# Expert pairs sorted once ahead of the expert loop, outputs stored as pair rows and fetched back by token

## The chip, the cores and the metric

One of the eight cores of a Trainium2 chip runs the whole program. The metric is device time in microseconds for one launch, taken as the median of several. Everything is float32; a few matmuls are done on float32 values split into a high and a low part in the narrower fp32r type.

## The reference, cut to what matters

Two layers work on 256 tokens of width 1024. Each has a token mixer and a channel mixer; the second layer's channel mixer is the one that is changed. It sends every token to the best two of eight experts, each a SwiGLU of inner width 3584:

```python
logits = t @ w_router + b_router
top_val, top_idx = lax.top_k(logits, 2)
gates = jax.nn.softmax(top_val)
# the 512 (token, expert) pairs are sorted by expert; then, for each expert's rows xblk:
yb = (silu(xblk @ w_gate_e[e]) * (xblk @ w_up_e[e])) @ w_down_e[e]
y[token] += gate_of_pair * yb
x = x + gate * rmsnorm(y, g_norm[1, 3])      # last norm and residual
```

Each expert's weights are 42 pieces of 1 MB (14 stages of gate, up and down), so all eight are 336 MB, read once.

## The kernel before

The first layer, the second mixer and the norm ahead of the experts keep the activations feature-major: `xT`, `hT` hold features on partitions and tokens along them. SyncE issues nothing but weight loads, in a fixed order, through a ring: 7 slots of 1 MB up to the experts, 14 slots (`ring_e`) for them. A slot is loaded again when `gu_full` or `down_done` says that its last reader is through (L650 and `last_use`).

**Routing.** PE computes the router's logits (L1103), transposes `hT` to token-major banks (L1108), and ScalarE copies these to `tok`. VectorE finds the two best experts of each token, the gates, and a token's rank within its expert by five small matmuls with a triangular matrix (L1114 to L1118). `cnt` then holds the number of tokens of each expert; `pos`, `Mm` and `Gm` hold ranks, membership and gates.

**The expert loop** is a real loop (`Fori`) of eight turns on PE, ScalarE and VectorE. Each engine loads `cnt[e]` into a register (L551 is the test that follows) and goes through nested `If`s to one of six bodies, for at most 32, 64, 128, 160, 192 or 256 tokens. A body of PE does, in this order:

- gather: VectorE has made a one-hot matrix `oh` (and one times the gates, `ohg`); PE multiplies `tok` by `oh` into four banks (L1146) and transposes `ohg` (L1152); ScalarE and VectorE copy the results to `mixT` and `gPT`;
- 14 stages, each once or twice (a block of 128 tokens and a rest): gate and up into a PG bank (L1176 for blocks under 128 rows, L1182 for 128), SiLU on ScalarE (L1253), the product on VectorE (L1955), a transpose by matmul (L1193), its copy (L1960), and the down product into Y (L1203). They are software-pipelined: the gate and up of a unit, the transpose of the one before it, the down product of the one before that;
- scatter: ScalarE and VectorE copy Y to `yeK` (L1253, L1966); PE multiplies `yeK` by `gPT` into four banks (L1226), and VectorE adds these to `yacc`, feature-major (L1971).

ScalarE's helper records all its operations as L1253. A semaphore wait stands ahead of each use of a bank or buffer.

**The end**: squares of `yacc`, their sum over partitions by matmul (L712, L717, L722), the root on GpSimd (L1992), gain and residual (L1567, L1571, L1997), 16 transposes to token-major (L1241), a copy to `tok`, and two stores by SyncE.

## Time and profile before

| what | value |
|---|---|
| median of 3 runs | 2094.73 us (2093.11 to 7076.81) |
| profiled execution | 2095.57 us, span 2093.8 us |
| PE busy | 1811.4 us, 87% of the span |
| VectorE, ScalarE, GpSimd busy | 443.5, 299.3, 43.1 us |
| bytes moved | 484.86 MB, mean 232 GB/s |
| expert loop | from 849.7 us to 2069.6 us |

The spans of the views are microseconds from the first instruction. "PE" is a matmul, "PEld" the load of its stationary operand; a float32 matmul call is recorded as two instructions. "issue" is time in which an engine waits for nothing that the profile shows. In the order of the loop the eight experts took the bodies for 32, 32, 128, 64, 160, 32, 192 and 64 tokens (read from the shapes of their matmuls). Here they are called E0 to E7. A "boundary" is the stretch from the end of an expert's last down product to the start of the next expert's first gate product.

### The profile page before, as it was taken

The numbers are of one execution on the slowest core, as the hardware profiler recorded it, in microseconds if no ns is written. First come the engines' busy times: TensorE is split into PE (matmuls) and PEld (weight loads), VectorE is DVE, ScalarE is ACT, GpSimd is POOL, SyncE is SP. The second block draws the span as 40 slices with busy tenths as digits, with TensorE's granted clock in tenths as the row PEclk, the third lists the DMA queues.
The fourth block names the chain that finished last, engine by engine and source line by source line (L and its number), as shares of the span: only waits on it lengthen the run. The fifth ranks groups of instructions, "written<-read, shape, count | busy, mean of one in ns | idle before, by whom it ended". The sixth has DMA issues, their size and how long they took to land.

```text
span 2093.8 us, 32178 instructions
## 1 busy us (share of the span) xinstructions
PE 1811.4 (87%) x13586; PEld 1349.1 (64%) x13587; DVE 443.5 (21%) x971; ACT 299.3 (14%) x585; POOL 43.1 (2%) x48
## 2 busy tenths in 40 slices
PE   3998979999899897665679979699997689999796
PEld 2776759999776676554467755477665466666453
DVE  1152235555415222111010011110011010000112
ACT  1222133333212211101000000100000010000101
POOL 0010000000001001000000000000000000000000
PEclk7997689999998767878789989799997889999797
DMA  6732357555342135599977759946463974444393
GB/s 235 286 121 80 149 188 286 183 183 189 131 147 110 75 155 223 240 419 402 420 316 288 297 205 417 388 164 240 196 241 159 420 318 181 181 181 181 112 418 139
DMA packets 75639, 484.86 MB, mean 232 GB/s; under 512 B 11872, under 2 KB 16236, under 8 KB 17516
## 3 DMA queue, kind: packets, MB, share of 16 engines
q1 hardware_dynamic: 71616, 478.02, 57.5%
q10 hardware_dynamic: 3756, 3.39, 0.6%
q8 instruction: 155, 2.54, 0.5%
q14 instruction: 112, 0.92, 0.1%
HBM read 480.33 MB, written 1.05 MB: 230 GB/s over the span
## 4 chain that ended last, share of the span: by engine, by line
PE 82%; issue 7%; DMA 5%; DVE 3%; ACTq 1%; ACT 1%; POOL 1%; SPq 0%; DVEq 0%; POOLq 0%
PE PG L1182 14%; PE Y L1203 13%; PE PG L1176 11%; DMA arena<-in_experts 5%; PE Y L796 4%; PE TRB L1193 3%; PE Y L804 3%; PE TRB L736 3%; PE Y L1049 3%; PE PG L760 3%; PE PG L762 3%; PE PG L761 3%; PE PG L1226 2%; PE TRB L1146 1%; PE TRB L1226 1%
## 5 line engine op out<-in xcount | busy, mean ns | idle before, releaser
L1960 DVE COPY arena<-TRB 128x64 f32<-128x64 f32 (+2 forms) x140 | 42.6, 305 | 835.4 <-PE TRB L1193 835.4
L1253 ACT ACTIVATE arena<-PG 128x256 f32<-128x256 f32 (+2 forms) x168 | 57.8, 344 | 1019.8 <-PE PG L1176 513.8
L1176 PE MATMUL PG<-ring,mixT 128*32 128x128 f32 (+1 forms) x2640 | 159.8, 320 | 28.2 <-issue 26.5
L1176 PE MATMUL PG<-arena,mixT 128*32 128x128 f32 (+1 forms) x2288 | 146.2, 336 | 36.3 <-issue 36.3
L1203 PE MATMUL Y<-arena 128*32 128x256 f32 (+2 forms) x896 | 171.6, 489 | 3.4 <-issue 3.4
L1176 PEld LDWEIGHTS PG<-ring,mixT 128*32 128x32 f32 (+1 forms) x2640 | 119.3, 124 | 75.3 <-issue 51.3
L1182 PE MATMUL PG<-ring,mixT 128*128 128x256 f32 x720 | 160.7, 381 | 1.3 <-DVE mixT L1943 1.3
L1176 PEld LDWEIGHTS PG<-arena,mixT 128*32 128x32 f32 (+1 forms) x2288 | 108.6, 131 | 78.5 <-issue 58.5
L1182 PEld LDWEIGHTS PG<-ring,mixT 128*128 128x128 f32 x720 | 135.4, 190 | 29.3 <-issue 11.9
L1182 PE MATMUL PG<-arena,mixT 128*128 128x256 f32 x624 | 139.9, 380 | 0.0
L760 PE MATMUL PG<-h_parts,parts 128*128 128x256 f32 x448 | 126.8, 283 | 10.0 <-DVE parts L1854 10.0
L1182 PEld LDWEIGHTS PG<-arena,mixT 128*128 128x128 f32 x624 | 117.0, 189 | 26.5 <-issue 10.2
L1203 PE MATMUL Y<-ring,arena 128*32 128x256 f32 (+2 forms) x672 | 127.9, 482 | 1.9 <-issue 1.9
L762 PE MATMUL PG<-h_parts,parts 128*128 128x256 f32 x448 | 126.8, 283 | 0.0
L761 PE MATMUL PG<-h_parts,parts 128*128 128x256 f32 x448 | 125.6, 280 | 0.0
L1146 PE MATMUL TRB<-arena,tok 128*128 128x128 f32 (+2 forms) x128 | 32.3, 446 | 89.3 <-issue 89.3
L1203 PEld LDWEIGHTS Y<-arena 128*32 128x32 f32 (+2 forms) x896 | 60.8, 134 | 71.5 <-issue 58.5
L1854 DVE TENSOR_TENSOR parts<-ring,parts 128x2048 fp32r<-128x2048 f32 x42 | 95.9, 2292 | 25.7 <-ACT parts L1253 25.7
L796 PE MATMUL Y<-hT,ring 128*128 128x256 f32 x416 | 95.3, 390 | 0.0
L760 PEld LDWEIGHTS PG<-h_parts,parts 128*128 128x128 f32 x448 | 85.4, 191 | 10.8 <-DVE parts L1854 10.4
L1146 PEld LDWEIGHTS TRB<-arena,tok 128*128 128x128 f32 x128 | 30.0, 330 | 94.0 <-issue 94.0
L1193 PEld LDWEIGHTS TRB<-con,arena 128*128 128x128 f32 (+1 forms) x448 | 62.8, 191 | 42.5 <-issue 40.5
(295 smaller groups left out, 2230.4 us busy)
## 6 DMA issues: line engine op xcount, KB each, us to landing
ring<-in_experts SPq DMA_DIRECT2D x168, 1024.0 KB, 9.1
arena<-in_experts SPq DMA_DIRECT2D x168, 1024.0 KB, 15.5
ring<-in_weights SPq DMA_DIRECT2D x116, 1024.0 KB, 6.3
ring<-in_weights SPq DMA_DIRECT2D x4, 512.0 KB, 4.0
tok<-in_x ACTq DMA_DIRECT2D x1, 1024.0 KB, 13.7
result<-tok SPq DMA_DIRECT2D x2, 512.0 KB, 2.8
ring<-in_weights SPq DMA_DIRECT2D x2, 432.0 KB, 6.2
arena<-in_w_ukv ACTq DMA_DIRECT2D x2, 384.0 KB, 4.2
```

What stands on the lines that cost most here:

```text
L736: last = mm(bank[32 * c:32 * c + 32, 0:SW], ccol[:, k, :], ring[:, slot_of[u], k, :], start=(k == 0), stop=(k == KD - 1))
L760: mm(out_, w_hi[w][:, c], x[0], start=first, stop=False, skip_group_check=True)
L761: mm(out_, w_hi[w][:, c], x[1], start=False, stop=False, skip_group_check=True)
L762: return mm(out_, w_lo[w][:, c], x[0], start=False, stop=last, skip_group_check=True)
L796: last = mm(bank_part, ring[:, s, k, c:c + m], hT[:, k, :], start=(k == 0), stop=(k == KD - 1))
L1146: last = mm(bank[:, j * T:j * T + w], tok[:, b, k * P:(k + 1) * P], oh[:, b, 0:w], start=(b == 0), stop=(b == TB - 1))
L1176: last = mm(bank[i * m:(i + 1) * m, 0:width], x[:, k, :], w[c // SW][:, k, c % SW:c % SW + width], start=(k == 0), stop=(k == KD - 1))
L1182: last = mm(bank[:, i * SW:(i + 1) * SW], x[:, k, :], w[i][:, k, :], start=(k == 0), stop=(k == KD - 1))
L1193: last = mm(tr[u % 2][:, f * P:(f + 1) * P], actK[r, u % 2, f * P:(f + 1) * P], ident[r, :], start=True, stop=True)
L1203: last = mm(o, actT[:, u % 2, f, 0:m], w[:, f, c:c + width], start=(s == 0 and f == 0), stop=(s == STAGES - 1 and f == 1))
L1226: last = mm(bank[:, q * T:(q + 1) * T], yeK[0:m, j, k * P:(k + 1) * P], gPT[0:m, j, :], start=(j == 0), stop=(j == len(bl) - 1))
L1854: V.tensor_tensor(w_lo[d % SPLITS], ring[:, slot_of[slot_of_dense(d)], :, :].rearrange("p k c -> p (k c)"), w_hi[d % SPLITS].bitcast(F32), ...
```

## The change

The pairs are ranked over all experts at once: `first[e]` is an exclusive sum of the counts, `slot` a pair's row among 512. The sorted activations `xs` (feature-major, 8 x 512 columns) are made before the loop by one product of `htok_hi` and `htok_lo` (the token-major activations split in two) with the 0/1 matrix `sel`, 32 matmuls of 512 columns, copied out by ScalarE and VectorE. In the loop GpSimd copies the expert's 256 columns of each of the 8 feature tiles from `xs` to `xe` (the buffer of `mixT`), once the expert before has done its last gate product. There is no gather, no transposed gate matrix and no scatter; the down outputs go to `yeK` and from there, by a DMA that ScalarE issues at a register's offset, to a DRAM scratch `ypairs`. `yeK` lies in `hT`'s buffer, and the first down product of an expert waits until the expert before has been copied out. After the loop GpSimd fetches two rows for each token with four indirect DMAs; ScalarE and VectorE weight and add them, and the last norm and residual are done token-major. The router's product runs in four column groups with a second small product that adds them. Slots of the ring, the six bodies and the loads of weights stay.

```diff
@@ tensor
-            for b in range(TB):
-                for k in range(KD):
-                    ...
-                    last = mm(bank[:, b * NE:(b + 1) * NE], hT[:, k, b * P:(b + 1) * P], wr[:, k, :], ...)
+            for k in range(KD):
+                pe.wait_ge(h_ready, 3 * KD + k + 1)
+                g = 32 * (k % 4)
+                last = mm(bank[g:g + 32, 0:T], wr[:, k, :], hT[:, k, :], start=(k < 4), stop=(k >= 4))
...
+            bank = take_tr("logit")
+            pe.wait_ge(*tr_done("router"))
+            for b in range(TB):
+                last = mm(bank[:, b * NE:(b + 1) * NE], s4[:, b * P:(b + 1) * P], strip_sum, start=True, stop=True)
...
             pe.wait_ge(htok_ready, 4)
+            pe.wait_ge(hlo_ready, 4)
+            pe.wait_ge(sel_ready, TB)
+            for k in range(KD):
+                f = slice(k * P, (k + 1) * P)
+                for b in range(TB):
+                    mm(xg_banks[k], htok_hi[:, b, f], sel[:, b, :], start=(b == 0), stop=False)
+                    last = mm(xg_banks[k], htok_lo[:, b, f], sel[:, b, :], start=False, stop=(b == TB - 1))
+                last.then_inc(xg_full, 1)
+            pe.wait_ge(xs_ready, KD)
+            pe.wait_ge(table_ready, 1)
+            pe.sem_inc(ye_ready, 2)
             with pe.Fori(0, NE) as e:
...
-                    pe.wait_ge(hot_ready, e * 1 + 1)
-                    for i in range(4):
-                        ...  (gather: mm(bank, tok, oh))
-                    for b in range(TB):
-                        ...  (transpose of ohg)
+                    pe.wait_ge(xe_ready, e + 1)
...
                         pe.wait_ge(at_ready, at_own(e, n, u))
+                        if s == 0:
+                            pe.wait_ge(ye_ready, e * 2 + 2)
...
-                    pe.wait_ge(ye_ready, e * 2 + 2)
-                    for i in range(4):
-                        ...  (scatter: mm(bank, yeK, gPT))
-            stats("post", 3, 7)
...
+            for b in range(TB):
+                for k in range(KD):
+                    last = nc.tensor.transpose(xtok_banks[b][k // 4][...], xT[:, k, b * P:(b + 1) * P], ident)
+            pe.wait_ge(ye_ready, 2 * NE + 2)
+            pe.wait_ge(diag8_ready, KD)
+            for k in range(KD):
+                last = mm(Y[:, k // 4, ...], ones[:, :], diag8[:, k, :], start=True, stop=True)
@@ scalar
+            for k in range(0, KD, 2):
+                ae.wait_ge(xg_full, k + 1)
+                run(xs[:, k * PAIRS:(k + 1) * PAIRS], xg_banks[k], ACT.Copy).then_inc(xs_ready, 1)
             with ae.Fori(0, NE) as e:
                 n_tok = ae.value_load(cnt[0:1, bass.ds(e, 1)], min_val=0, max_val=T)
+                start = ae.value_load(first[0:1, bass.ds(e, 1)], min_val=0, max_val=PAIRS)
...
                     ae.wait_ge(down_done, e * FT + 2 * FT)
+                    for b in range(TB):
+                        ae.wait_ge(y_stored[b], e * 16 + 16)
                     ...  (yeK copies)
                     last.then_inc(ye_ready, 1)
+                    ae.wait_ge(ye_ready, e * 2 + 4)
+                    for j, m in blocks(n):
+                        ae.dma_start(ypairs[bass.ds(start + j * P, m), :], yeK[0:m, j, :]).then_inc(y_stored[j], 16)
...
+            for b in range(TB):
+                ae.wait_ge(y_back[b], 32)
+                run(y1[:, b, :], y1[:, b, :], ACT.Copy, scale=gt2[:, b, 0:1]).then_inc(y1_scaled, 1)
+            for b in range(TB):
+                ae.wait_ge(y_summed, b + 1)
+                run(mixT[...], y2[:, b, :], ACT.Square, accum_out=msq[:, b:b + 1]).then_inc(ysq_ready, 1)
@@ vector
+            V.tensor_tensor(Mm, oh[:, :, 0, :], oh[:, :, 1, :], ALU.add).then_inc(routed, 1)
+            for q in range(4):
+                ve.wait_ge(htok_ready, q + 1)
+                V.tensor_tensor(htok_lo[...], Y[:, q, :], htok_hi[...], ALU.subtract).then_inc(hlo_ready, 1)
+            ...  (counts, scan to `upto`, pos, cnt, first, ohp, slot: some ten small operations)
+            for b in range(TB):
+                mark(V.tensor_scalar(sel[:, b, :], iota, slot[:, 2 * b:2 * b + 1], None, ALU.is_equal))
+            for b in range(TB):
+                V.scalar_tensor_tensor(sel[:, b, :], iota, slot[:, 2 * b + 1:2 * b + 2], sel[...],
+                                       ALU.is_equal, ALU.add).then_inc(sel_ready, 1)
...
+            for k in range(1, KD, 2):
+                V.tensor_copy(xs[:, k * PAIRS:(k + 1) * PAIRS], xg_banks[k]).then_inc(xs_ready, 1)
...
-                    one_hot(e + 1)
-                    for i in range(6, 10):
-                        ...  (yacc += bank)
-            post(3)
+            for b in range(TB):
+                V.scalar_tensor_tensor(y2[:, b, :], y2[:, b, :], gt2[:, b, 3:4], y1[:, b, :], ALU.mult, ALU.add)
+            ...  (mean square)
+            for b in range(TB):
+                ...  (y1 = y2 * rstd * gain, two halves; y1 += xT transposed, two halves)
@@ gpsimd
+            for k in range(KD):
+                G.tensor_scalar(diag8[:, k, :], ident, gg[:, 3, k:k + 1], None, ALU.mult).then_inc(diag8_ready, 1)
+            with po.Fori(0, NE) as e:
+                start = po.value_load(first[0:1, bass.ds(e, 1)], min_val=0, max_val=PAIRS)
+                po.wait_ge(gu_full, e * FT + FT)
+                src = xs[:, bass.ds(start, KD * PAIRS)].rearrange("p (k s) -> p k s", k=KD)
+                G.tensor_copy(xe[:, :, :], src[:, :, 0:T]).then_inc(xe_ready, 1)
+            for b in range(TB):
+                po.wait_ge(y_stored[b], 16 * NE + 16)
+            for b in range(TB):
+                for c, to in enumerate((y1, y2)):
+                    po.indirect_dma_start(to[:, b, :], None, ypairs[0:PAIRS, :], ...).then_inc(y_back[b], 16)
+            for b in range(TB):
+                G.tensor_tensor(rstd[:, b:b + 1], msq[:, b:b + 1], half[:, 0:1], ALU.pow).then_inc(end_rstd, 1)
```

## Rows read from the trace of the kernel before

**Rows 1.** Stretches: from:to, length, busy PE, PEld, DVE, ACT, POOL, PEclk, DMA share, GB/s.
```profile
880.00:930.00 50.00, 32.38 (x594) 24.11 (x598) 3.64 (x14) 1.89 (x7) 0.00 (x0) 0.80 1.01 420
1070.00:1210.00 140.00, 140.00 (x585) 106.91 (x586) 10.58 (x29) 6.28 (x14) 0.00 (x0) 1.00 0.73 284
1240.00:1330.00 90.00, 89.07 (x646) 52.14 (x645) 12.58 (x36) 7.80 (x19) 0.00 (x0) 0.98 0.89 366
1700.00:1940.00 240.00, 239.50 (x1221) 154.88 (x1221) 23.89 (x62) 12.67 (x32) 0.00 (x0) 1.00 0.47 185
```

**Rows 2.** Chain that ended last: start, length, what; from E0 to E2.
```profile
1008.25 25.91 DMA arena<-in_experts
...
1043.28 1.91 PE Y L1203 x32
...
1050.08 10.43 issue
1060.51 3.77 PE TRB L1146 x16
...
1069.76 10.26 PE PG L1182 x46
```

**Rows 3.** The same chain, from the end of E6 to the start of E7.
```profile
1941.51 5.53 PE Y L1203 x16
...
1956.07 9.20 PE PG L1226 x16
...
1980.55 4.50 PE PG L1176 x39
```

**Rows 4.** Groups by line over the expert loop: busy us, mean ns, idle before by releaser.
```profile
L1146 PE MATMUL TRB<-arena,tok 128*128 128x128 f32 (+2 forms) x128 | 32.3, 446 | 89.3 <-issue 89.3
...
L1253 ACT ACT_TABLE_LOAD x15 | 19.2, 1283 | 117.7 <-issue 89.6 <-PE PG L1176 20.4 <-PE PG L1182 7.6
```

**Rows 5.** Timeline from the router to E0's first gate product.
```profile
826.60 6.97 PE L1103 MATMUL TRB<-wr,hT 128*128 128x8 f32 x32 [1.67 <-ACT hT L1253]
...
837.10 2.06 ACT L1253 ACTIVATE tok<-Y 128x512 f32<-128x512 f32 x4 [2.35 <-PE Y L1108]
...
849.68 3.78 PE L1146 MATMUL TRB<-arena,tok 128*128 128x128 f32 x16 [10.98 <-issue]
...
856.61 3.66 PE L1176 MATMUL PG<-ring,mixT 128*32 128x128 f32 x123 [0.40 <-DVE mixT L1943]
...
858.76 0.86 SPq L650 DMA_DIRECT2D ring<-in_experts  x2
```

**Rows 6.** Timeline of boundaries, with the idle time before each: E3 to E4, E5 to E6.
```profile
1329.58 0.69 DVE L1966 COPY arena<-Y 64x512 f32<-64x512 f32 x1 [3.25 <-PE Y L1203]
...
1343.90 1.28 ACT L1253 ACT_TABLE_LOAD   x1 [13.74 <-issue]
...
1351.86 4.63 PE L1146 MATMUL TRB<-arena,tok 128*128 128x160 f32 x16 [16.70 <-issue]
...
1693.33 5.15 PE L1146 MATMUL TRB<-arena,tok 128*128 128x192 f32 x16 [8.81 <-issue]
```

**Rows 7.** The chain between E4 and E5, VectorE's way to its next body.
```profile
1584.39 2.93 issue
...
1587.45 3.42 issue
```

**Rows 8.** Stretches: the fp32r matmuls of the dense layer; before E0.
```profile
400.00:500.00 100.00, 100.00 (x847) 100.00 (x846) 53.22 (x53) 36.49 (x30) 0.00 (x0) 1.00 0.51 182
840.00:850.00 10.00, 0.32 (x1) 0.33 (x2) 0.40 (x2) 1.28 (x1) 0.00 (x0) 0.56 0.05 11
```

**Rows 9.** Groups of GpSimd by form.
```profile
L2016 POOL COPY arena<-scr 32x1536 f32<-32x1536 f32 x2 | 2.9, 1456 | 57.7 <-DVE scr L1697 57.7
```

**Rows 10.** The chain at the end: E7's last down products.
```profile
2060.72 3.61 PE Y L1203 x16
```

**Rows 11.** DMA issues: queue, count, KB each, median us to landing.
```profile
result<-tok SPq DMA_DIRECT2D x2, 512.0 KB, 2.8
```

More of the change, by code:

```diff
@@ L69, in const_table @@
     t[:, C_MK:C_MK + P] = np.where(i[None, :] < CHUNK, 0.0, NEG)
-    t[:, C_IOTA:C_IOTA + T] = np.arange(T)
+    t[:, C_IOTA:C_IOTA + PAIRS] = np.arange(PAIRS)
+    for e in range(NE):
+        t[e:P:32, C_SEL + e] = 1.0
     for m in range(CR // 2):
@@ L238, in rs_names, with build @@
     return names
-def build(nc, ap, out):
+def build(nc, ap, out, ypairs):
     uses = weight_uses()
@@ L386, in build @@
         h_hi, h_lo = h_parts[:, 0, :, :], h_parts[:, 1, :, :]
-        yacc = cut("ffn", KD, T)
+        sel_at = top["ffn"]
+        sel = parts[:, sel_at:sel_at + TB * PAIRS].rearrange("p (b s) -> p b s", b=TB)
+        diag8 = cut("ffn", KD, P)
         sgK = cut("ffn", 2, SW)
@@ L399, in build @@
         gt2 = cut("ffn", TB, 4)
-        oh1 = cut("ffn", TB, NE)
-        oh2 = cut("ffn", TB, NE)
-        Gm = cut("ffn", TB, NE + 1)
-        Mm = cut("ffn", TB, NE + 1)
-        pos = cut("ffn", TB, NE + 1)
+        oh = cut("ffn", TB, 2, NE)
+        ohp = cut("ffn", TB, 2, NE)
+        Mm = cut("ffn", TB, NE)
+        pos = cut("ffn", TB, NE)
+        total = cut("ffn", NE)
+        upto = cut("ffn", NE)
+        zero8 = cut("ffn", NE)
+        slot = cut("ffn", 2 * TB)
+        msq = cut("ffn", TB)
+        rstd = cut("ffn", TB)
+        xe = mixT
+        yeK = hT.rearrange("p k t -> p (k t)").rearrange("p (b d) -> p b d", b=TB)
+        htok_hi, htok_lo = (h_parts[:, i, :, :].rearrange("p k t -> p (k t)").rearrange("p (b d) -> p b d", b=TB) for i in range(2))
+        y1 = scr.rearrange("p k t -> p (k t)").rearrange("p (b d) -> p b d", b=TB)
+        y2 = tok
         ring_e = [ring[:, (n_before + i) % SLOTS, :, :] for i in range(SLOTS)] + [cut("ffn", KD, SW) for _ in range(SLOTS_E - SLOTS)]
@@ L502, in build @@
         htok_ready = sem("htok_ready")
-        hot_ready = sem("hot_ready")
-        ax_full = sem("ax_full")
-        ax_free = [sem(f"ax_free{i}") for i in range(4)]
+        hlo_ready = sem("hlo_ready")
+        table_ready = sem("table_ready")
+        sel_ready = sem("sel_ready")
+        xg_full = sem("xg_full")
+        xs_ready = sem("xs_ready")
+        pad_zero = sem("pad_zero")
+        xe_ready = sem("xe_ready")
+        y_stored = [sem(f"y_stored{i}") for i in range(TB)]
+        y_back = [sem(f"y_back{i}") for i in range(TB)]
+        diag8_ready = sem("diag8_ready")
+        end_full = sem("end_full")
+        y1_scaled = sem("y1_scaled")
+        y_summed = sem("y_summed")
+        ysq_ready = sem("ysq_ready")
+        msq_ready = sem("msq_ready")
+        end_rstd = sem("end_rstd")
         tp_full = sem("tp_full")
@@ L607, in tr_done @@
             return tr_free[TR.bank(name)], TR.before(name) + 1
-        tr_before_experts = [TR.before(x) + 1 for x in ("router", "rank")]
-        if TR.bank("router"):
-            tr_before_experts.reverse()
         block = ctx.enter_context(nc.Block())
```

262 lines of the change are left out of this document (115 added, 147 removed).

## The prediction

> **What bounds the kernel now.** I read the stretches first. In the loop two things alternate. Inside E2, E3, E4, E6 and E7 PE is busy without a break while the DMA engines are not full: 140.00 of 140 us at a DMA share of 0.73 in E2, 89.07 of 90 at 0.89 in E3 [rows 1]. Inside E0, E1 and E5, the bodies for 32 tokens, PE is busy 32.38 of 50 us and the DMA engines all the time, at 420 GB/s [rows 1]; there the chain of waits passes through the landing of weights, 25.91 us at one go [rows 2]. At that rate an expert's 42 pieces take 42 x 1.0486 / 0.42 = 105 us. The loop of eight takes some 1214 us, 8 x 105 would be 840: outside the small experts the weights are no bound.
>
> Next I read the chain at the boundaries. From the end of E1's last down product (1045.19) to E2's first gate product (1069.76) pass 24.6 us [rows 2]; from E6's (1947.04) to E7's (1980.55) 33.5 [rows 3]. The six boundaries from E1/E2 to E6/E7 take 24.6, 24.4, 30.2, 33.6, 23.9 and 33.5, together 170.2 us. PE-bound experts follow or precede each of them, or (E5) one that can't load ahead further than its 14 slots, so a boundary's length is on the path. The seventh, E0/E1, isn't: the DMA engines are full from E0's start to E1's end.
>
> Of a boundary, one part is PE idle for "issue": 89.3 us over eight entries to a body [rows 4], of which 11.0 before E0 [rows 5] and 15.9 before E1, so 62.5 in the six, 8.8 to 16.7 each except one of 4.5 [rows 6]. It is the way through the loop's end, the register load and the nested tests: on VectorE between E4 and E5 the chain shows four stops, the first two of 2.93 and 3.42 us and the others like them, one for each jump [rows 7]. The rest, 170.2 - 62.5 = 107.7 us, is gather, scatter and their copies.
>
> The Trainium skill (Runtime: NRT & Kernel Launch, Instruction fetch mechanics) says that a taken branch out of the two pages held makes the sequencer fetch the target first; the four stops agree. Its page Advanced Engine Details and Errata (Control Flow Timing) gives about 51 ns for a branch and 108 ns for a compare and branch; if that were all, a boundary would be some 12 us shorter than in my sum and the time about 1950. Every entry in the trace speaks against it.
>
> **The boundaries after the change.** The jumps stay: same loop, same six bodies, on PE, ScalarE and VectorE. PE starts its jumps as soon as the last down product is issued. Its bounds are the idle times seen, 8.8 and 16.7 us [rows 6]. The lower ones flatter it: PE's sequencer had queued the scatter's products (up to 9.20 us of them [rows 3]) and was jumping while they ran, and now only the last down product, 1 to 3.5 us, covers it. ScalarE, which had no such lead, took 13.74 us from its last copy to its first instruction of the next body [rows 6], and 89.6 over the seven boundaries [rows 4], 12.8 each. I take 12.5 us for PE. Then gate products start at once, on a PE that has idled: its clock is 0.56 over such a gap [rows 8], and the first 16 gather products took 3.77 us at 1.2 GHz before the rate went up [rows 2]. Up to now the gather paid for that; now the gate products lose half of it, 1.9 us.
>
> ScalarE's new work: wait for both halves of `yeK`, issue one or two DMAs (0.43 us each, as SyncE's issues: 0.86 for two [rows 5]), a second register load. It leaves about 2 us after PE's last product, needs 12.8 us for its jumps and 1.28 for a table [rows 6], so SiLU 0 can be done about 16.5 us after it. PE needs it only for the transpose of unit 0, behind two units of gate products: 12.5 plus 4 to 14 us. A lateness of 0.5 us on average goes into the sum (0 for the 128-row bodies, up to 3 for the small). VectorE is no later.
>
> GpSimd's copy of `xe` moves 2048 elements a partition: 1456 ns for 1536 [rows 9] give 2 us. It starts at the last gate product, at least 4.5 us before the last down product ends, so 12.5 + 4.5 us cover it; without that cover it would cost 2 us a boundary. The waits for `ye_ready` before the first down product and for `y_stored` before the copies (from the store of the expert before, 80 us or more back) cost nothing for the same reason. The stores, 2 MB in all, are 5 us of DMA time, nearly all where the engines have room.
>
> New length: 12.5 + 1.9 + 0.5 = 14.9, times six 89.4. **Saved: 170.2 - 89.4 = 81 us.** At 8.8 a boundary it would be 103, at 16.7 it would be 56.
>
> Does this turn back into waiting for weights? E3 needs 3 pieces per 6 us stage against 2.4 arriving, with 14 ahead: 14 + 2.4 x 13 = 45 for 42. E4 then begins with about 8 instead of 14, at 14.7 us a stage: enough. E5 starts with a full ring as now. Nothing is given back.
>
> **Ahead of the loop.** The DMA engines are idle, share 0.05 [rows 8], until E0's first gate product frees a slot (858.76 [rows 5]), and E0 and E1 run on the weights from there: whatever is added here shifts everything. Router: 6.97 us of 32 recorded instructions [rows 5] become 8 calls in four column groups, bounded by the arrival of `hT`, about 3.5 us less; the transposes, unchanged, and two small products bring the logits to VectorE at 834.4, 0.8 later than now. One-hots and `routed`: 836.4. ScalarE's four copies (2.06) end at 838; VectorE subtracts the low parts, 4 x 0.69 us (0.69 for 512 columns on VectorE [rows 6]), till 839.3; some ten small operations till 841.1; `sel`, four of 512 columns at 0.6 to 0.7, till 843.8. Then 32 products of 512 columns. 847 fp32r instructions of 256 columns took 100 us [rows 8], 0.118 each, so 0.236 at full clock and 0.47 at half. About 4 us at half, the rest at full: 9.4 us (bounds 7.5 and 15), and 0.6 for the last copy: 854. Only now PE and the others enter the loop: 10.5 us of jumps, as before E0 now [rows 5], under which GpSimd's eight small operations and first copy (4 us) are hidden. E0's first gate product: 864.5 instead of 856.6, and the first slot free 1.7 us later for the half clock. **Added: 9.5 us** (bounds 5 and 16).
>
> **The end.** Now 2093.8 - 2064.3 = 29.5 us follow the last down product [rows 10]. New: copies 0.7; issue and landing of the store 3.3 (2.8 for 512 KB [rows 11]); four indirect DMAs of 512 KB on GpSimd. None is in the trace: bounds 2.8 us if they overlap wholly, 4 x 2.8 + 4 = 15 if they don't; I take 7.5, as their bytes need 5 us at 420 GB/s. Then scale 1.0, square 2.0, VectorE's sum 1.2, root 0.7 and five or six 512-wide pairs at 1.4 on two blocks, 6 in all, store 3.2. Sum 25.6: **saved 4 us** (from -8 to 9). The Trainium skill (DMA: Bandwidth & Descriptors, Anatomy of one DMA) has about 2.0 us plus bytes at 436 GB/s for a DMA of GpSimd; 2 MB would be 6.8 us by it, an estimate, and the sum would hardly move.
>
> **Sum.** The profiled execution took 2095.57 us, 0.8 above the median. 2095.6 - 81 + 9.5 - 4 = 2020.
>
> **Rivals.**
> - *The jumps get longer.* Scatter and gather spread the engines' jumps apart; now three engines jump within 2 us of one another, fetch at once, and the slowest decides, at 16.7 plus lateness of ScalarE up to 3. Six boundaries at 19: 2020 + 25 = 2045. For: entries of 15.9 and 16.7 stand where the DMA engines were busy. Against: 8.8 stands there too. 20%.
> - *The jumps get shorter*: PE's queue covers more, 8.8 a boundary: 1998. 10%.
> - *The gain comes back as waiting for weights* in E3 to E5, 30 us of it: 2050. Against: the count of pieces. 6%.
> - *Slower: the row fetches.* If GpSimd builds each row's descriptor one by one, the end grows with 512 rows. It decides from (2020 to 2137) 117 us, 0.23 us a row; at 0.25 the time is 2020 + 128 - 7 = 2141. No row here has an indirect DMA, so it can't be excluded. 3%.
> - *My forecast*: 2000 to 2042, 61%.
>
> **Numbers.** 2020; range 1992 to 2052, from the short jumps to the long ones with the bounds of prologue and end. A measurement tells about 2% from no change, 2053 here. Faster: 0.61 + 0.10 + 0.15 of the long jumps + 0.04 = 0.90; same 0.07; slower 0.03.
>
> **What would show it.** Right: no 30 us boundaries; six of 11 to 18 us with a single "issue" stop; clock 0.5 over the first 4 us of each body; weights' landing still ends the waits in E0, E1, E5; first slot freed near 868. Wrong: PE waiting for ScalarE or VectorE at unit 0 by more than 3 us, stops well outside 8.8 to 16.7, waits for weights in E3 or E4, more than 40 us after the last down product.

## The result: 2.4% faster, 26 us less than forecast

The changed kernel takes 2046.16 us (median of four runs, 2040.29 to 2046.67), the kernel before beside it 2094.4: a ratio of 0.9755, 95% interval 0.9741 to 0.9769 (the two medians by themselves divide to 0.977; one execution of the kernel before, of 7076.81 us, stands outside the ratio). The forecast was 2020 in 1992 to 2052, and "faster". The profiled execution took 2046.35 us, its span 2044.6 against 2093.8.

### Where the span went

Four instants cut both traces: the router's first product, E0's first gate product, the end of the last down product, the end of the span.

| stretch | before | after | change | predicted |
|---|---|---|---|---|
| start to router | 826.6 | 831.6 | +5.0 | 0 |
| router to E0's first gate product | 30.0 | 36.2 | +6.2 | +7.9 |
| E0's first gate to E7's last down product | 1207.7 | 1150.5 | -57.2 | -79 |
| of it: the six boundaries | 170.3 | 101.8 | -68.5 | -81, with the slower start of each body |
| of it: inside the bodies, and E0/E1 | 1037.4 | 1048.7 | +11.2 | +1.7 |
| last down product to the end | 29.5 | 26.3 | -3.2 | -4 |

Chain of waits after, start, length, what; the lines that answer to [rows 2, 3], then those of the other boundaries:

```profile
1061.97 10.75 issue
1072.72 15.83 PE PG L1189 x64
...
1225.75 13.36 issue
1239.11 9.31 PE PG L1183 x64
...
1324.94 18.75 issue
...
1551.82 18.14 issue
...
1653.48 13.58 issue
1667.06 8.62 PE PG L1189 x32
...
1913.20 19.68 issue
1932.88 8.88 PE PG L1183 x64
```

Where there were a stop, a gather, copies, and at the end a scatter ([rows 2, 3]: 24.6 and 33.5 us), there is one stop and nothing else. Two of the lines are shorter than the boundary, because at its start the chain runs through the landing of the last weights (E1/E2, E5/E6); from product to product the six take 13.2, 13.4, 18.8, 18.1, 18.7 and 19.7 us, mean 17.0.

Waits of PE after, over the loop (868 to 2018 us): engine, line, what for: total, times, longest:

```profile
PE PG L1183 <- issue: 152.6, 33, 20.1
PE PG L1189 <- issue: 50.6, 3, 18.8
PE Y L1212 <- issue: 3.9, 3, 1.6
PE TRB L1200 <- DVE arena L1954: 0.4, 1, 0.4
PE Y L1212 <- DMA arena<-in_experts: 0.2, 1, 0.2
```

That is the whole list. PE hardly waits for ScalarE, VectorE or GpSimd anywhere in the loop, and outside "issue" it shows one wait for weights, of 0.2 us. (In the 32-token bodies a wait for a slot's weights hides under "issue", as in the 62.8 us of L1176 before; the chain shows it as a DMA.)

Timeline after, the boundary E3/E4 of [rows 6]: start, length, engine, line, operation, and in brackets the idle time before:

```profile
1326.01 0.62 ACTq L1492 DMA_DIRECT2D ypairs<-hT  x1
1342.10 1.28 ACT L1246 ACT_TABLE_LOAD   x1 [16.38 <-issue]
...
1343.70 9.95 PE L1189 MATMUL PG<-ring,mixT 128*128 128x256 f32 x32 [18.75 <-issue]
```

From its last copy ScalarE does nothing for 16.4 us but issue its store and jump, and it stands in the next body 1.6 us before PE. Before, the same way took it 13.74, and PE, which could start jumping while the scatter ran, 16.70 [rows 6].

Timeline after, from the router to the first freed slot, the lines that answer to [rows 5]:

```profile
831.64 3.76 PE L1123 MATMUL TRB<-hT,wr 128*32 128x256 f32 x16 [1.67 <-ACT hT L1246]
...
839.72 2.04 ACT L1246 ACTIVATE h_parts<-Y 128x512 fp32r<-128x512 f32 x4
...
845.41 1.41 DVE L1927 SCALAR_TENSOR_TENSOR parts<-con,arena,parts 128x512 fp32r<-128x512 f32 x2
...
847.04 0.77 PE L1153 MATMUL PG<-parts,h_parts 128*128 128x512 f32 x1 [4.06 <-issue]
...
856.07 0.39 PE L1154 MATMUL TRB<-parts,h_parts 128*128 128x512 f32 x1
...
857.35 4.68 POOL L2062 TENSOR_SCALAR arena<-con,gg 128x128 f32<-128x128 f32 x8 [28.86 <-DVE arena L1944]
861.98 1.89 POOL L2067 COPY mixT<-arena 128x2048 f32 x1
...
867.82 5.48 PE L1183 MATMUL PG<-ring,mixT 128*32 128x128 f32 x128 [11.36 <-issue]
871.65 2.71 SPq L671 DMA_DIRECT2D ring<-in_experts  x4
```

Measured from the router's first product: router 3.76 us long (6.97 before, [rows 5]; I said 3.5 less), `sel` ready after 15.2 (said 17.2), 32 gather products in 9.4 us (said 9.4, about 4 us of it at the lower clock: they start every 0.42 us up to 851.0 and every 0.23 behind it), then 11.36 us from the last of them to E0's first gate product (said 11.1). GpSimd's eight small operations and first copy end 6.5 us after they began (said 4). The slot is freed 40.0 us after the router, 32.2 before: +7.9, said +9.5.

Chain of waits after, the end, the lines behind [rows 10]:

```profile
2014.70 3.61 PE Y L1212 x16
...
2019.36 2.99 DMA ypairs<-hT
...
2022.64 1.21 POOL scr L2072
2024.15 0.94 POOL tok L2072
...
2026.64 5.65 DMA tok<-ypairs,row_of
2032.31 1.16 ACT scr L1246
```

A row fetch of 128 rows is issued in 0.94 us (the first 1.21); the last lands 5.65 us behind the start of its issue; four take 9.7 us, overlapped. I took 7.5.

Stretches after (from:to, length, busy PE, PEld, DVE, ACT, POOL, PEclk, DMA share, GB/s): the inside of E0, E2, E3 and E6, as in [rows 1], and the first 4 us of E4:

```profile
895.00:945.00 50.00, 32.03 (x575) 24.73 (x576) 3.64 (x14) 1.88 (x7) 1.28 (x1) 0.80 1.01 420
1085.00:1225.00 140.00, 140.00 (x568) 103.28 (x567) 10.25 (x27) 4.99 (x13) 1.90 (x1) 1.00 0.75 299
1245.00:1325.00 80.00, 79.94 (x584) 43.80 (x580) 10.07 (x28) 6.55 (x15) 1.90 (x1) 1.00 1.00 409
1343.70:1347.70 4.00, 4.00 (x10) 3.19 (x11) 0.00 (x0) 0.00 (x0) 0.00 (x0) 0.50 1.03 420
...
1700.00:1900.00 200.00, 200.00 (x1000) 128.13 (x999) 17.95 (x46) 8.74 (x23) 0.00 (x0) 1.00 0.46 182
```

PE is busy 140.00 of 140 us in E2 and 79.94 of 80 in E3, where the DMA share is now 1.00 instead of 0.89: the margin I counted for E3 is used up, and no wait has come of it. In E0 the weights are the bound as before, at 420 GB/s. A body begins at a granted clock of 0.50, the level of 1.2 GHz, as forecast.

### The profile page after: what moved, and what is told of

The parts are those of the page before. It is cut to its first block, busy times and chain, and to the rows that moved or that the text cites. A ratio compares the mean times of both kernels' runs of the same rounds, so it can differ in the third digit from the quotient of the medians.

```text
span 2044.6 us, 31233 instructions
## 1 busy us (share of the span) xinstructions
PE 1716.0 (84%) x13162; PEld 1278.3 (63%) x13163; DVE 409.3 (20%) x887; ACT 283.9 (14%) x553; POOL 62.8 (3%) x67
## 4 chain that ended last, share of the span: by engine, by line
PE 77%; DMA 8%; issue 8%; DVE 3%; ACT 1%; ACTq 1%; POOL 1%; SPq 0%; POOLq 0%; DVEq 0%
PE PG L1189 15%; PE Y L1212 13%; PE PG L1183 11%; DMA ring<-in_experts 6%; PE Y L817 4%; PE TRB L1200 3%; PE Y L825 3%; PE Y L1070 3%; PE PG L781 3%; PE PG L782 3%; PE PG L783 3%; PE TRB L757 2%; DMA arena<-in_experts 1%; PE Y L783 1%; PE Y L782 1%
## 5 line engine op out<-in xcount | busy, mean ns | idle before, releaser
L1183 PE MATMUL PG<-ring,mixT 128*32 128x128 f32 (+1 forms) x2640 | 171.1, 339 | 113.3 <-issue 113.3
L1183 PEld LDWEIGHTS PG<-ring,mixT 128*32 128x32 f32 (+1 forms) x2640 | 128.5, 133 | 165.5 <-issue 141.7
L1189 PE MATMUL PG<-ring,mixT 128*128 128x256 f32 x720 | 166.7, 391 | 50.6 <-issue 50.6
L1189 PEld LDWEIGHTS PG<-ring,mixT 128*128 128x128 f32 x720 | 139.9, 196 | 81.1 <-issue 61.9
L781 PE MATMUL PG<-h_parts,parts 128*128 128x256 f32 x448 | 128.0, 286 | 10.2 <-DVE parts L1848 10.2
L782 PE MATMUL PG<-h_parts,parts 128*128 128x256 f32 x448 | 127.7, 285 | 0.0
L783 PE MATMUL PG<-h_parts,parts 128*128 128x256 f32 x448 | 127.6, 285 | 0.0
L781 PEld LDWEIGHTS PG<-h_parts,parts 128*128 128x128 f32 x448 | 86.9, 194 | 10.8 <-DVE parts L1848 10.4
L1954 DVE TENSOR_TENSOR arena<-PG,arena 64x128 f32<-64x128 f32 (+2 forms) x140 | 52.1, 372 | 190.1 <-ACT arena L1246 185.5
L1200 PE MATMUL TRB<-con,arena 128*128 128x128 f32 (+1 forms) x448 | 87.6, 307 | 0.4 <-DVE arena L1954 0.4
## 6 DMA issues: line engine op xcount, KB each, us to landing
ring<-in_experts SPq DMA_DIRECT2D x168, 1024.0 KB, 10.5
arena<-in_experts SPq DMA_DIRECT2D x168, 1024.0 KB, 16.3
```

The source lines that it names most:

```text
L781: mm(out_, w_hi[w][:, c], x[0], start=first, stop=False, skip_group_check=True)
L782: mm(out_, w_hi[w][:, c], x[1], start=False, stop=False, skip_group_check=True)
L783: return mm(out_, w_lo[w][:, c], x[0], start=False, stop=last, skip_group_check=True)
L1183: last = mm(bank[i * m:(i + 1) * m, 0:width], x[:, k, :], w[c // SW][:, k, c % SW:c % SW + width], start=(k == 0), stop=(k == KD - 1))
L1189: last = mm(bank[:, i * SW:(i + 1) * SW], x[:, k, :], w[i][:, k, :], start=(k == 0), stop=(k == KD - 1))
L1200: last = mm(tr[u % 2][:, f * P:(f + 1) * P], actK[r, u % 2, f * P:(f + 1) * P], ident[r, :], start=True, stop=True)
```

## The experiments

The question was why the stop at a boundary is 17.0 us on average and not 12.5, and what the whole change is worth apart from it. My theory: a stop is the fetch of code over jumps, back to the head of the loop and through the nested tests to the body; TensorE's sequencer makes it while the products already in its queue run, and in the kernel before these were the scatter's. Rivals: the engines fetch at one another's cost since they jump together; PE waits for another engine; the DMA queues are busy with weights.

"Boundary" in what follows is from the end of the last down product to the next first gate product, "stop" the longest idle time of PE within it. This table is worked out from the matmul records of each profiled execution; us. Two executions of one kernel give the spread of a boundary: 0.3 us at most between after and changed_again, but up to 1.4 between unrolled_early and early_again.

| kernel | E1/E2 | E2/E3 | E3/E4 | E4/E5 | E5/E6 | E6/E7 | six stops | six boundaries |
|---|---|---|---|---|---|---|---|---|
| before | 10.4 | 12.9 | 16.7 | 4.5 | 8.8 | 9.1 | 62.5 | 170.3 |
| no_scatter | 14.3 | 13.3 | 18.3 | 16.3 | 13.2 | 18.4 | 93.8 | 136.8 |
| no_gather | 10.8 | 13.7 | 17.7 | 8.8 | 7.8 | 13.6 | 72.5 | 134.3 |
| before_unrolled | 1.6 | 12.6 | 10.3 | 5.0 | 3.1 | 4.6 | 37.2 | 137.5 |
| after | 13.2 | 13.4 | 18.8 | 18.1 | 18.7 | 19.7 | 101.8 | 101.8 |
| changed_again | 13.2 | 13.4 | 18.5 | 18.4 | 18.5 | 19.6 | 101.6 | 101.6 |
| others_unrolled | 13.3 | 13.2 | 18.3 | 17.5 | 18.4 | 19.6 | 100.3 | 100.3 |
| quarter_weights | 9.9 | 9.8 | 13.2 | 13.8 | 12.5 | 14.4 | 73.6 | 73.6 |
| unrolled | 7.5 | 12.8 | 10.7 | 17.8 | 5.7 | 14.0 | 68.5 | 68.5 |
| warm | 6.5 | 8.3 | 13.8 | 7.7 | 6.3 | 11.2 | 53.7 | 137.1 |
| unrolled_early | 6.2 | 12.8 | 12.3 | 17.3 | 6.4 | 14.0 | 68.9 | 68.9 |
| early_again | 7.5 | 13.6 | 10.9 | 18.1 | 6.2 | 13.9 | 70.2 | 70.2 |
| early_idle6 | 1.6 | 11.4 | 6.5 | 12.0 | 2.3 | 10.3 | 44.2 | 76.1 |

### changed_again: the changed kernel once more

> The changed kernel once more, as the base of this group. Both theories: 2040 to 2047 us. The stretch ahead of the router began 5.0 us later in its first trace than before the change (831.64 against 826.60); if that is the state of TensorE's clock in the first 60 us and not the change, it moves by some us here; if it is the change, it stays at 831 to 832. PE's idle time at the six boundaries: 101.7 us in the first trace (13.2, 13.4, 18.8, 18.1, 18.7, 19.7).

2047.07 us, ratio 0.9763 (0.974 to 0.9787), stops as in the first trace within 0.3 us. The router starts at 828.6 us instead of 831.6. In three profiled executions of kernels with the old code ahead of the router it starts at 826.6 and in a fourth (no_gather) at 828.0, mean 826.9; in nine with the new code (the first trace among them) at 825.6 to 831.6, mean 829.2. So about half of the +5.0 us of the first comparison is that one execution. The means differ by 2.3 us, less than the nine are apart from one another; whether that is the change stays open.

### no_scatter: the kernel before without its scatter

```diff
@@ tensor: ahead of the first down product
+                        if s == 0:
+                            pe.wait_ge(ye_ready, e * 2 + 2)
...
-                    pe.wait_ge(ye_ready, e * 2 + 2)
-                    for i in range(4):
-                        bank = take()
-                        ... last = mm(bank[:, q * T:(q + 1) * T], yeK[0:m, j, ...], gPT[0:m, j, :], ...)
-                        last.then_inc(ax_full, 1)
@@ vector
-                    for i in range(6, 10):
-                        ... V.tensor_tensor(o, o, bank..., ALU.add).then_inc(free, 1)
```

> The kernel before the change without the scatter: the products with gPT and the additions to yacc are left out, gather and all else stay, and the first down product waits for the copies as in the changed kernel. Theory A (the scatter's queued products covered the jumps): PE's stops from E4 to E5 and E6 to E7, 4.5 and 9.1 us before, become 17 to 20 us, the others grow by 1 to 3 us, and of 58 us of scatter at the six boundaries only about 25 to 30 show: 2062 to 2072 us. Theory B (the stops in the changed kernel are longer because three engines jump at one time, and gather still comes ahead of the gates here): also longer, so it tells less here. Theory C (the stops are of fixed length, 10.4 us on average): 2094 - 58 = 2036 us.

2056.56 us, ratio 0.9818 (0.9801 to 0.9834), 5 us under the range of theory A (2062 to 2072). Chain of waits, the boundaries E2/E3 and E4/E5:

```profile
1219.61 13.35 issue
1232.96 3.78 PE TRB L1147 x16
...
1555.03 16.33 issue
1571.37 3.78 PE TRB L1147 x16
```

The boundaries lose 33.5 us and the six stops grow by 31.4 (62.5 to 93.8), in the old kernel, with nothing of the change in it. Where the scatter was longest (E4/E5, E6/E7: 9.20 us for its products, [rows 3]) the stop grows most, 4.5 to 16.3 and 9.1 to 18.4; at E2/E3 by only 0.4. That is the failed term: about half of what was removed (31.4 of 33.5 + 31.4) had been running under a fetch of code. The insides of E2, E3, E4, E6 and E7 are unchanged (151.5, 83.8, 205.6, 245.0, 83.8 us); the gather still comes first and takes the lower clock on itself.

### no_gather: the kernel before without its gather

```diff
-                    for i in range(4):
-                        bank = take()
-                        ... last = mm(bank[:, j * T:j * T + w], tok[:, b, ...], oh[:, b, 0:w], ...)
-                        last.then_inc(ax_full, 1)
@@ scalar, vector
-                    ... the copies of these four banks to mixT
```

> The kernel before the change without the gather's 16 products of tok and their copies; the transposes of the gate matrix and the scatter stay, the experts work on old activations. Theory A (scatter's queue covers the jumps, gather doesn't): PE's stops keep their lengths, 62.5 us in the six boundaries, and what goes is the gather alone, 7 to 8 us per boundary and once ahead of E0, less 1 to 2 us of half clock each: 2094 - 7 x 6 = 2052, range 2045 to 2060 us. Theory B (stops are longer when work behind them is short): PE's stops grow here too, as in the run without scatter.

2074.51 us, ratio 0.9896 (0.9879 to 0.9912): 15 us over the range that I gave (2045 to 2060). The profiled execution is the fastest of the five, 2064.13 us where the other four took 2073.0 to 2075.8, so its trace shows 10 us more of a gain than the time does, and where the others lost these 10 us isn't recorded.

In this trace the boundaries lose 36.0 us and the six stops grow by 10.0 (62.5 to 72.5), 4.3 at E4/E5 and 4.5 at E6/E7, so theory A, by which the stops keep their lengths, holds for the other four boundaries alone. The bodies behind them get longer by 1.8, 2.5, 1.9, 1.5 and 1.5 us (E2, E3, E4, E6, E7): this is the price of beginning at half clock, 1.9 on average, and my 1.9 was right. Together with no_scatter the boundaries lose 33.5 + 36.0 = 69.5 us; in the changed kernel they lose 68.5. The traces' two parts add up to what the change does at a boundary. By the times they can't be added in this way, since no_gather's trace isn't its typical execution.

### warm: 16 idle products behind each expert

```diff
                     ... (after the last down product)
+                    for i in range(16):
+                        mm(PG[:, i % 2, :], ident, con[:, 0:512], start=True, stop=True)
```

> The changed kernel with 16 products of 512 columns, whose results nobody reads, behind the last down product of every expert: 13.7 us of PE work at full clock that lies in PE's queue while its sequencer goes to the next body. Theory A (the jumps run beneath queued work; scatter used to be that cover, and gather the warm-up of the clock): the start of the next gate product doesn't move, PE's real idle time at the six boundaries falls from 102 to 20-35 us, and the first two units of gate products run at full clock where the remaining gap is short: 5 to 15 us gained, 2031 to 2041 us. Theory B (the sequencer can't go on while the queue is that full, or jumps only after the queue is empty): every boundary grows by about 13 us, six of them on the path: 2046 + 80 = 2126 us.

2080.77 us, ratio 0.9932 (0.9916 to 0.9949), 34 us more than the changed kernel and between the two theories (2031 to 2041, and 2126). Timeline of PE at E2/E3:

```profile
1229.61 13.90 PE L1225 MATMUL PG<-con 128*128 128x512 f32 x32
1251.77 8.60 PE L1183 MATMUL PG<-ring,mixT 128*64 128x256 f32 x60 [8.26 <-issue]
```

16 products take 13.7 us. The stop behind them is 5.1 us shorter here (13.4 to 8.3) and 8.0 on average (101.6 to 53.7 over six), from 4.8 at E3/E4 to 12.2 at E5/E6. If the fetch began with the queue dry, it would not be shorter at all; if all 16 ran under the fetch, the boundaries would not have grown, and they grew by 35.5 us. So the queue hides a part of such products. How much it holds can't be told from this: the 16 products also make the code longer, and 32 blocks of it are fetched in the six boundaries where the changed kernel fetches 27 or 28 (what a block is stands under unrolled). My further hope, that the products save the clock, failed: the gate products after them run at a granted clock of 0.51 over the first 4 us and take 8.60 us for 60 records, 0.143 each, against 0.115 once the clock is up (32 of them in 3.67 us).

### others_unrolled: the loop written out on ScalarE, VectorE and GpSimd

```diff
-            with ae.Fori(0, NE) as e:
+            for e in range(NE):
@@ the same on VectorE and GpSimd; TensorE keeps its loop
```

> The changed kernel with the expert loop written out on ScalarE, VectorE and GpSimd but kept on PE. Theory A (each engine's way is its own, and PE's is the one that decides): PE's stops and the time as in the changed kernel, 2044 to 2050 us. Theory B (three engines jump at one time and fetch at each other's cost, or PE waits for the slowest): at least half of the 36 us that writing out all of them gave, 2030 us or less.

2040.99 us, ratio 0.9735 (0.9714 to 0.9756), no different from the changed kernel's 0.9763. DMA queues of the page (packets, MB, share), first of the changed kernel, then of this one:

```profile
q8 instruction: 150, 2.46, 0.5%
...
q14 instruction: 106, 0.87, 0.1%
```

```profile
q8 instruction: 150, 2.46, 0.5%
...
q14 instruction: 58, 0.48, 0.1%
```

### unrolled: written out on all four

```diff
-            with pe.Fori(0, NE) as e:
-                n_tok = pe.value_load(cnt[0:1, bass.ds(e, 1)], min_val=0, max_val=T)
+            for e in range(NE):
+                n_tok = pe.value_load(cnt[0:1, e:e + 1], min_val=0, max_val=T)
@@ and the same on ScalarE, VectorE and GpSimd
```

> The changed kernel with the loop over the experts written out eight times on PE, ScalarE, VectorE and GpSimd (the tests for the six bodies stay, SyncE's loop stays). Theory A (a boundary is a number of fetches of far code, 3 to 6 blocks at about 3.5 us each; the way back to the loop's head is one of them on PE): one fetch less, PE's six stops fall from 102 to about 80 us: 2022 to 2030 us. Theory B (the time is in the register load and the tests themselves, or in waits for the other engines): no change within 0.3%. Theory C (more code, worse fetches): slower by up to 1%.

2010.87 us, ratio 0.9594 (0.9578 to 0.961): the gain is larger than theory A had it (2022 to 2030 us, stops of 80). The six stops fall from 101.6 to 68.5. DMA traffic around the boundary E6/E7 (packets, MB, share of that window), of the changed kernel and of this one:

```profile
q8 instruction: 6, 0.10, 3.0%
```

```profile
q8 instruction: 4, 0.07, 2.6%
```

A packet of q8 is a block of 16 KB. Six blocks of code in a stop of 19.7 us, four in one of 14.0. Over the six boundaries I count 27 blocks in 101.8 us and 19 in 68.5: 3.8 and 3.6 us a block. That is an average (3.2 to 5.7 from boundary to boundary): the packets themselves take 0.9 to 2.4 us, and some start in pairs less than 0.6 us apart. The stop follows the number of blocks fetched, and a third of it goes with the jump back to the loop's head. That third is uneven: 12.8 us at E5/E6 and 7.9 at E3/E4, but 0.6 at E2/E3 and at E4/E5. The rest is the way through the tests to the body, and it depends on which body is left and which entered: 5.7 us (one block) from 32 to 192 tokens, 17.8 (five) from 160 to 32.

### quarter_weights: less traffic beside the fetches

```diff
-                slot = ring_e[i % SLOTS_E].rearrange("p k c -> p (k c)")
+                c = KD * SW if full else KD * SW // 4
+                slot = ring_e[i % SLOTS_E].rearrange("p k c -> p (k c)")[:, 0:c]
@@ the first 14 pieces are still loaded whole
```

> The changed kernel with only the first quarter of every expert weight piece loaded after the first 14 pieces (the products read stale data): the DMA engines are nearly idle at every boundary. Theory A (the stops are a number of fetches of far code, each some 3.5 us, whatever else the DMA engines do): PE's six stops stay within 5 us of 101.6, and only E0, E1 and E5 get shorter, by 25 to 35 us each: about 1950 us. Theory B (fetches wait behind weight pieces of 1 MB): the stops where the DMA engines were full (into E1, E2, E4, E6) shrink by 5 us or more each, the others don't: 1930 us or less.

One execution, 1908.05 us; most of the gain is E0, E1 and E5, which no longer wait for weights (47.2, 48.8, 48.3 us instead of 79.4, 92.2, 78.4). The stops fall to 73.6 us, which is neither theory: they shrink by 28 us and not by under 5, and at all six boundaries (3.3 to 6.2 us) and not only at those with full DMA engines. The blocks are about as many, 28 with five that start within the last microsecond before the stop, 23 without them: 2.6 or 3.2 us a block instead of 3.8.

Two things shrink, about half each. From the first of these fetches to the gate product the six boundaries take 72.0 us instead of 85.7 in the first trace of the changed kernel, and 12.1 of these 13.7 us are at E1/E2, E3/E4 and E5/E6, where the DMA engines were full (share 1.01 to 1.02 over the stop, 0.34 to 0.71 at the other three). The other 14.5 us are fetches that begin earlier against the last down product; why they do stays open. So the DMA queues' load is a third cause, about 28 us of the 102. It was there before the change too. At the three boundaries that are not full the share over the stop is somewhat higher in the changed kernel than in no_scatter (0.71, 0.50, 0.34 against 0.61, 0.42, 0.23), so a small part in the difference isn't excluded.

### unrolled_early and early_again: a later wait, and `diag8` built behind the loop

Both are the written-out kernel with this edit:

```diff
-            pe.wait_ge(xs_ready, KD)
             pe.wait_ge(table_ready, 1)
...
                     pe.wait_ge(xe_ready, e + 1)
+                    pe.wait_ge(xs_ready, KD)
@@ gpsimd: the eight operations that make diag8 moved from ahead of the loop to behind it
```

> The written-out kernel (2010.9 us), in which PE no longer waits for xs ahead of the first test but behind it, and GpSimd builds diag8 after its last copy and not before its first. Theory A: E0's first gate product began 11.4 us after the last gather product although xe had been ready 3.9 us earlier; now the jumps start up to 2 us earlier under queued gather products and xe is ready 4.7 us earlier, so E0 starts 2 to 5 us earlier: 2006 to 2009 us. Theory B (the way into the first body starts only when PE's queue has drained): no change, 2010 to 2012 us.

> The kernel of unrolled_early once more, as the base for the next kernel on the same chip. Nothing new is asked of it: ratio to before 0.958 +- 0.003, boundaries 13.2, 6.2, 12.8, 12.3, 17.3, 6.4 and 14.0 us, each within 0.7.

2008.2 us, ratio 0.9583 (0.9567 to 0.9599), and once more 2010.91, 0.959 (0.957 to 0.9611). E0's first gate product stands 30.6 us behind the router in both, close to the kernel before (30.0) and not at 35.3 as in unrolled; the stop ahead of it is 6.0 and 5.8 us instead of 10.5. E1 ends 4.3 us earlier, counted from the router. The time can't show it: a gain of that size is 0.2%, no more than the intervals are wide, and the second set of runs is level with unrolled. Of the boundaries that I expected of early_again within 0.7 us, four came out 0.8 to 1.4 away (E1/E2, E2/E3, E3/E4, E4/E5). This is the most the experiments got out of the design, 1.8% under the changed kernel and 4.1% under the one before.

### early_idle6: six idle products

The kernel of early_again with this behind each expert's last down product:

```diff
+                    for i in range(6):
+                        mm(PG[:, i % 2, :], ident, con[:, 0:512], start=True, stop=True)
```

> unrolled_early with six products of 512 columns into a free accumulator behind each expert's last down product (six at 0.86 us are 5.1 us; their result is not used). Theory (a stop is a count of code fetches that TensorE's sequencer makes while its queue drains, and the queue hides what is still to run in it): the six products run under the fetches, so a boundary stays as long as without them (sum of the last six 68.9, now 66 to 71), the stop behind them is 5 us shorter than the boundary, and where the boundary was about 6 us (E2, E6) TensorE hardly pauses, so the first gate products run at full clock and E2 and E6 gain 1 to 2 us each: 2003 to 2008 us. Rival (products cost their time, the fetch begins only when the queue has run dry): each boundary is 5.1 us longer, 35 us in all, 2043 us.

2010.59 us, ratio 0.9597 (0.9581 to 0.9614). The stops fall from 70.2 to 44.2, the boundaries grow from 70.2 to 76.1: of 31 us of idle products 25 cost nothing, which is the theory's side; 5.9 did cost, more than I allowed (66 to 71), and the time is 2.6 us above my range. The 5.9 need not be the queue's limit: at E2/E3, E5/E6 and E6/E7, 2.9, 1.5 and 1.8 us longer, the trace has one block of code more than in early_again (5, 2 and 5 instead of 4, 1 and 4), and the other three differ by 1.0, -0.6 and -0.7. Stretches, first E1/E2 (the end of the idle products' side, then the gate products), then E5/E6:

```profile
1057.00:1061.00 4.00, 4.00 (x21) 3.51 (x20) 0.00 (x0) 0.00 (x0) 0.00 (x0) 1.00 1.02 412
...
1629.00:1633.00 4.00, 1.73 (x5) 0.42 (x3) 0.00 (x0) 0.00 (x0) 0.00 (x0) 1.00 1.00 395
1633.00:1637.00 4.00, 3.93 (x12) 3.24 (x13) 0.00 (x0) 0.00 (x0) 0.00 (x0) 0.63 1.02 422
```

E2's gate products (first line, from 1054.64 on, behind a stop of 1.58 us) run at clock 1.00, and 64 records take 14.05 us instead of 15.83. At E6, behind a stop of 2.34 us, the clock is 1.00 in the stretch with the stop and 0.63 in the next. So my expectation held for one of two, and the time shows no gain.

### before_unrolled: the kernel before, written out

```diff
-            with pe.Fori(0, NE) as e:
+            for e in range(NE):
@@ and the same on ScalarE and VectorE
```

> The kernel before with its expert loop written out eight times on TensorE, ScalarE and VectorE (the same instructions in the same order, no jump back). In the kernel before the stop by issue lay behind the gather and before the scatter's products (8.8, 9.2, 5.5 us and so on, six together 62.5), and no_scatter showed 93.8 for six when nothing stood in front. Theory (the jump back costs fetches, the scatter covers part): six stops fall by 20 to 33 us as unrolling took 33 from the changed kernel, as far as the cover leaves it to gain: 2060 to 2075 us, ratio 0.983 to 0.991, and against it the whole worth of the change, both written out, is 0.967 to 0.975. Rival A (the stop in the kernel before is not the jump back but the branch to a body in the switch): no stop shorter, 2094 us. Rival B (written-out code is longer and each body is fetched anew, so more fetches fall inside the bodies): 2095 to 2110 us.

2058.15 us, ratio 0.9817 (0.9801 to 0.9834), 2 us below the range that I gave. Waits of PE, total, times, longest, of the kernel before and of this one:

```profile
PE TRB L1146 <- issue: 89.3, 8, 16.7
PE PG L1176 <- issue: 62.8, 27, 4.1
```

```profile
PE PG L1176 <- issue: 67.8, 26, 4.3
PE TRB L1146 <- issue: 58.1, 8, 12.6
```

The eight entries to a body lose 31 us (L1146), the six boundaries 32.8, the time 37. Both rivals are out: the jump back was part of the stop in the old kernel as well, and writing the code out doesn't lengthen the bodies behind the six boundaries (151.5, 84.3, 205.6, 79.5, 245.0, 83.8). It also says what the change is worth without loops: 0.959 / 0.9817 = 0.977, as with them (0.9755, 0.9763). Jump back and scatter are two prices that add: writing the loop out takes 33 us off the six boundaries with and without the scatter (170.3 to 137.5, 101.6 to 68.5). And from before_unrolled to unrolled the stops grow by 31.3 us (37.2 to 68.5), so the cover is there without the jump back too.

## Why the prediction was right, and where it was 26 us off

The direction and the range held, the range with 6 us to spare. Four of the six stops are over 18 us, outside the 11 to 18 that I gave as a sign of being right. By the prediction's own steps:

- **The boundary is on the path and shrinks by gather, scatter and copies: right.** All six shrink, and in the traces no_gather and no_scatter give the same 69 us between them.
- **The stop, 12.5 us: the failed size.** It measured 17.0, so 27 us less gain. 107.8 us of gather, scatter, copies and waits went from the six boundaries; I let the stops grow by 12.5 us for it (62.5 to 75), and they grew by 39. The step that failed is the one that took ScalarE's 12.8 us for PE. The prediction said that the low entries (8.8) flattered PE since the scatter had covered its jumps, but then it took a value from the middle of the covered ones. no_scatter has 15.6 on average once the cover is away. Of the other 8.0 us, 5.5 are one boundary, E5/E6 (13.2 without the scatter, 18.7 in the changed kernel), and there the traces show why: fetches start 2.8, 8.7, 10 and 16 us after the last down product in both, but in no_scatter the gather's first product starts at 13.2, and the fourth fetch runs under the gather; in the changed kernel nothing runs, and it ends the stop. So the gather, too, had covered a fetch. DMA queues (packets, MB, share) from the last down product to the first product of the next body, of no_scatter and of the changed kernel:

```profile
q8 instruction: 3, 0.05, 1.7%
```

```profile
q8 instruction: 4, 0.07, 1.6%
```

- **The rival of longer jumps** had each boundary at 19 us, stop, half clock and lateness together, and the time at 2045; measured are 18.8 (17.0 and the 1.8 below) and 2046, so its numbers were nearer than mine. Its reason, engines in one another's way, is refuted as a cause of that size by others_unrolled. The short-jump rival is refuted by the stops.
- **Half clock, 1.9 us a body: right.** 1.9 by no_gather, 1.8 in E2, E3, E4, E6 and E7 of the changed kernel, at a granted clock of 0.50 in the first 4 us. Its bodies E2 to E7 grew by 8.1 us in sum instead of 11.4, since E5, which waits for weights, took up its share and 0.8 more.
- **ScalarE's lateness, 0.5 us a body: not there.** No wait of PE for ScalarE in the loop; its 16.38 us of jumps end before PE's. 3 us too much.
- **The copy of `xe` and the waits for `ye_ready` and `y_stored` cost nothing: right** in the loop; no wait stands behind them.
- **Nothing is given back as waiting for weights: right.** E0 and E1 took 3.2 us more, 1.7 forecast.
- **Ahead of the loop, +9.5: measured +7.9.** Gather and clock came out at their forecast lengths, routing 2 us shorter. The way into E0's body did too, 11.36 against 11.1, but not for the reason given: GpSimd's work under it took 6.5 us and not 4, and unrolled_early, which moves that work and a wait, makes the way 4.5 us shorter.
- **The end, -4: measured -3.2.** Fetches 9.7 us instead of 7.5, the pieces behind them 12.3 instead of 14.1. The row fetches, the only rival with a slower kernel, cost 0.94 us of issue per 128 rows, 0.007 us a row where 0.23 was the point of decision.
- **Ahead of the router, 0: measured +5.0** in this pair of executions, 2.0 in the next.

In sum 26.8 (stops) - 3.3 (half clock) - 3.0 (lateness) + 5.0 (ahead of the router) - 1.7 (router to E0) + 1.5 (E0 and E1) + 0.8 (end) = 26.1 of the 26.3 us between forecast and profiled time; the rest is rounding. That the miss is no larger than the stops' is luck: +5.0 and -6.3 of other terms nearly cancel.

The Trainium skill (Runtime: NRT & Kernel Launch, Instruction fetch mechanics) says that a taken branch whose target isn't among the pages held makes the engine fetch that page before it goes on, and that this is a reason to unroll. The runs agree: one to six blocks in each stop, and 36 to 37 us less when the loop is written out. The length of such a stop comes from the runs alone: on average 3.6 to 3.8 us a block beside the full weight traffic and 2.6 to 3.2 beside a quarter of it. The figures of the Trainium skill, Advanced Engine Details and Errata (Control Flow Timing), some 51 ns for a branch and 108 ns for a compare and branch, do not describe a stop of 13 to 20 us, as the prediction already held.

## What to carry to other kernels

Before you count an engine's products as time to be saved, look at what its sequencer does while they run: if a jump to other code follows them, the products in its queue hide the fetch, and taking them away gives back only what exceeds it. Here no_scatter took 65 us of scatter, copies and waits out of six boundaries and got 31 back as stops; the whole change took out 108 and got 39 back. And take a stop without cover from an entry without cover. The cheaper gain lay beside the change: a loop of a few turns over large bodies is better written out, where that fits.

## What was not expected of the hardware

- An uncovered way from one body to the next costs TensorE 13 to 20 us in the loop and 6 to 18 written out, with one to six blocks of 16 KB fetched, on average 3.6 to 3.8 us each; 2.6 to 3.2 with a quarter of the weight traffic, in one execution.
- TensorE's sequencer goes on past its running products: of 16 float32 products of 512 columns, 13.7 us, 8.0 us were hidden on average (4.8 to 12.2 by boundary), of six, 5.1 us, 4.3.
- Other engines' fetches cost TensorE's next to nothing: 51 to 28 of them in six boundaries, and the stops 101.6 to 100.3 us.
- The granted clock stayed at 1.00 over a stop of 1.58 us behind the idle products of E1/E2 and fell to 0.63 behind one of 2.34 us at E5/E6, both behind a body for 32 tokens.
- An indirect DMA of 128 rows of 4 KB is issued by GpSimd in 0.94 us and lands 4.7 to 5.7 us after its issue begins; four of them overlap to 9.7 us.
